# Late experts' one-hot products in fp32r: weighted matrix split high and low, built on GpSimd

## The reference, cut to what matters

```python
def block(xb):
    q = (xb @ w_query).reshape(PEER_TOKEN_BLOCK, PEER_HEADS, 2, D_KEY // 2)
    s = jnp.einsum('thpc,pkc->thpk', q, sub_keys).astype(jnp.float32)
    s1, i1 = lax.top_k(s[:, :, 0], PEER_TOPK)
    s2, i2 = lax.top_k(s[:, :, 1], PEER_TOPK)
    ...
    e = (jnp.take_along_axis(i1, ci // PEER_TOPK, axis=-1) * N_KEYS
         + jnp.take_along_axis(i2, ci % PEER_TOPK, axis=-1))
    g = jax.nn.softmax(sc, axis=-1)
    u = expert_u[e]
    act = jax.nn.gelu(jnp.einsum('td,thkd->thk', xb, u).astype(jnp.float32))
    return jnp.einsum('thk,thkd->td', (g * act).astype(xb.dtype), expert_v[e])
```

## Time and profile before

| what | before |
|---|---|
| runs shown | 1579.97, 1580.24, 1581.9 us; median 1580.24 |
| profiled execution | 1581.13 us, its span 1579.4 us |
| TensorE busy | 1535.6 us, 97% of the span |
| VectorE, ScalarE, GpSimd busy | 1158.2, 834.4, 298.4 us |
| late stage | 982.5 to 1223.6 us |

### The profile page before, as it was taken

One profiled execution on the slowest core, in us unless ns is written; L12 is line 12 of the kernel. 1 busy time (PEld: TensorE's weight loads), 2 busy tenths in 40 slices (PEclk: granted clock), 3 DMA queues, 4 the chain that ended last, 5 costly groups with the idle time before them and its releaser, 6 DMA issues.

```text
span 1579.4 us, 31066 instructions
## 1 busy us (share of the span) xinstructions
PE 1535.6 (97%) x10840; PEld 1431.5 (91%) x10840; DVE 1158.2 (73%) x2379; ACT 834.4 (53%) x1466; POOL 298.4 (19%) x418
## 2 busy tenths in 40 slices
PE   7999999999999999999999998999999999999998
PEld 7998787899899999889999998999999888888886
DVE  5799887765566666875999996888888665666664
ACT  5545678654544445564576675333333545454544
POOL 2010664000100000000000002888887000000000
PEclk9999999999999999999999999999999999999999
DMA  7573433543465554423455554444444656656663
GB/s 247 176 251 105 141 111 118 162 166 126 158 190 177 184 184 147 161 96 105 161 173 168 192 184 150 141 137 140 139 138 147 195 196 189 197 189 197 189 197 107
DMA packets 70860, 257.80 MB, mean 163 GB/s; under 512 B 8272, under 2 KB 8480, under 8 KB 70528
## 3 DMA queue, kind: packets, MB, share of 16 engines
q1 hardware_dynamic: 67824, 246.97, 48.1%
q0 software_dynamic: 2960, 9.86, 2.0%
HBM read 254.67 MB, written 1.08 MB: 162 GB/s over the span
## 4 chain that ended last, share of the span: by engine, by line
PE 84%; DVE 9%; ACT 4%; POOL 1%; issue 1%; DMA 0%; DVEq 0%; ACTq 0%; POOLq 0%
PE bank L362 17%; PE bank L363 17%; PE bank L364 17%; PE bank L940 7%; PE bank L941 7%; PE bank L939 7%; PE bank L918 4%; DVE arena L1642 2%; DVE ring_lo L1561 2%; POOL arena L1007 1%; ACT ring_hi L1065 1%; PE bank L446 1%; ACT arena L1199 1%; PE bank L430 1%; PE bank L432 1%
## 5 line engine op out<-in xcount | busy, mean ns | idle before, releaser
L1561 DVE TENSOR_TENSOR ring_lo<-ring_raw,ring_hi 128x1024 fp32r<-128x1024 f32 x460 | 564.5, 1231 | 187.3 <-ACT ring_hi L1065 184.6
L362 PE MATMUL bank<-operand_hi,ring_hi 128*128 128x256 f32 x2144 | 621.9, 290 | 16.4 <-DVE ring_lo L1561 8.4
L363 PE MATMUL bank<-operand_lo,ring_hi 128*128 128x256 f32 x2144 | 611.1, 285 | 0.0
L364 PE MATMUL bank<-operand_hi,ring_lo 128*128 128x256 f32 x2144 | 611.0, 285 | 0.0
L1065 ACT ACTIVATE ring_hi<-ring_raw 128x1024 fp32r<-128x1024 f32 x460 | 481.7, 1049 | 84.2 <-PE bank L364 70.0
L362 PEld LDWEIGHTS bank<-operand_hi,ring_hi 128*128 128x128 f32 x2144 | 416.3, 194 | 19.5 <-DVE ring_lo L1561 10.8
L363 PEld LDWEIGHTS bank<-operand_lo,ring_hi 128*128 128x128 f32 x2144 | 416.5, 194 | 0.2
L364 PEld LDWEIGHTS bank<-operand_hi,ring_lo 128*128 128x128 f32 x2144 | 415.7, 194 | 0.0
L1049 POOL TENSOR_SCALAR onehots<-iota_k,routeT 128x128 f32<-128x128 f32 x256 | 205.6, 818 | 586.4 <-ACT routeT L1483 544.2
L939 PE MATMUL bank<-ring_hi,hidden_hi 128*128 128x512 f32 x512 | 199.2, 389 | 0.0
L940 PE MATMUL bank<-ring_lo,hidden_hi 128*128 128x512 f32 x512 | 199.2, 389 | 0.0
(11 more groups left out here) (281 smaller groups left out, 1802.8 us busy)
## 6 DMA issues: line engine op xcount, KB each, us to landing
ring_raw<-in_stream SPq DMA_DIRECT2D x467, 512.0 KB, 3.6
arena<-bias_rows POOLq DMA_DIRECT2D x8, 384.0 KB, 4.2
arena<-in_memT SPq DMA_DIRECT2D x2, 512.0 KB, 5.1
arena<-in_xT POOLq DMA_DIRECT2D x1, 1024.0 KB, 9.1
arena<-in_w POOLq DMA_DIRECT2D x2, 512.0 KB, 10.5
arena<-in_memT POOLq DMA_DIRECT2D x1, 1024.0 KB, 5.3
out_rows<-arena SPq DMA_DIRECT2D x2, 512.0 KB, 2.6
arena<-arena POOLq DMA_DIRECT2D x4, 128.0 KB, 4.7
```

The lines of the kernel that those rows point to most:

```text
L362: pe.matmul(out, wh, xh, start=start, stop=False, **kw)
L363: pe.matmul(out, wh, xl, start=False, stop=False, **kw)
L364: return pe.matmul(out, wl, xh, start=False, stop=stop, **kw)
L1561: dve.tensor_tensor(w_lo[:, slot, 0:n], raw[:, slot, 0:n], (raw if n == 1 else w_hi)[:, slot, 0:n].bitcast(F32), ALU.subtract)\
```

## The change

The product is made of two fp32r products. The one-hot of i2 is exact in fp32r, so only the weighted one-hot of i1 is split.

- GpSimd now builds the weighted one-hots (compare and multiply in one instruction with two scalars per partition) into `weighted`, in plain f32. This shares its memory (the tile is named final_gain) with act_out, std, ident and ones_mean.
- ScalarE gets `split_hots(n + 2)`: the high part as fp32r, one instruction of 128x512, into h_hi (even blocks) or h_lo (odd ones). Those are free in this stage. It stands between `hi` and the GELUs and waits for GpSimd.
- VectorE builds the one-hots of i2 (128x512, one instruction) and, when the high part is there, the low part (128x512) in `build_hots`.
- TensorE: per token two products with the same stationary side. It waits for hot_ready alone.
- The copy of the weights of tiles not done moves from VectorE to ScalarE (`rest_of_block`), ahead of `hi`; gate_block waits for it.
- `build_hots` of block 1 is made ahead of the loop, as that of block 0. GpSimd's wait for the products of block n - 2 stays.

```diff
@@ build: tiles @@
-        hot = sb("onehots", [P, 2, TB, P])
+        hot = sb("onehots", [P, 2, TB, P], F32R)
...
+        with ExitStack() as shared:
+            fg = shared.enter_context(nc.sbuf_tensor("final_gain", [P, D], F32))
+        with ExitStack() as shared:
+            act2 = shared.enter_context(nc.sbuf_tensor("act_out", [P, 2, S], F32))
+            std = shared.enter_context(nc.sbuf_tensor("std", [P, S], F32))
+            ident = shared.enter_context(nc.sbuf_tensor("ident", [P, P], F32))
+            ones = shared.enter_context(nc.sbuf_tensor("ones_mean", [P, P], F32))
+        low = sb("weighted_lo", [P, 2, TB, P], F32R)
+        high = [h_hi[:].rearrange("p a (b i) -> p (a b) i", i=NEXP), h_lo[:].rearrange("p a (b i) -> p (a b) i", i=NEXP)]
...
-        row_hot = [[act_hot[:, j, :] for j in range(TB)], [std_hot[:, 0, :], std_hot[:, 1, :], ident[:], ones[:]]]
+        weighted = fg[:].rearrange("p (q t i) -> p q t i", q=2, t=TB)
@@ TensorE, weight_block(n, q, free) @@
                 pe.wait_ge(hot_ready, n + 1)
-                pe.wait_ge(hot_built, n + 1)
                 pe.wait_ge(bank_free[6 + q], free)
                 for j in range(TB):
-                    m = pe.matmul(bank[6 + q][:, j * NEXP:(j + 1) * NEXP], hot[:, q, j, :], row_hot[q][j],
-                                  start=True, stop=True)
+                    o = bank[6 + q][:, j * NEXP:(j + 1) * NEXP]
+                    pe.matmul(o, hot[:, q, j, :], high[q][:, j, :], start=True, stop=False)
+                    m = pe.matmul(o, hot[:, q, j, :], low[:, q, j, :], start=False, stop=True)
@@ GpSimd @@
-                    ins = pool.tensor_scalar(hot[:, q, j, :], iota_k[:], routeT[:, 1, token], None, ALU.is_equal)
+                    ins = pool.tensor_scalar(weighted[:, q, j, :], iota_k[:], routeT[:, 0, token], routeT[:, 2, token], ALU.is_equal, ALU.mult)
@@ ScalarE @@
+            def split_hots(n):
+
+                act.wait_ge(hot_built, n + 1)
+                act.activation(high[n % 2], weighted[:, n % 2, :, :], ACT.Copy).then_inc(hot_split, 1)
+
+            def rest_of_block(n):
+
+                act.wait_ge(wall_ps, n + 1)
+                w = bank[6 + n % 2][:, :].rearrange("p (t i) -> p i t", t=TB)
+                act.activation(wall[:, EARLY + n:NEXP, n * TB:(n + 1) * TB], w[:, EARLY + n:NEXP, :], ACT.Copy).then_inc(rest_kept, 1)
+
+            split_hots(0)
+            split_hots(1)
             for n in range(BLOCKS):
                 q = n % 2
                 gated = TB * (n + 1)
+                rest_of_block(n)
                 hi(u0 + n + 3, (u0 + n + 3) % RING)
+                if n + 2 < BLOCKS:
+                    split_hots(n + 2)
@@ VectorE @@
             def build_hots(n):
 
                 q = n % 2
-                if n >= 2:
-                    dve.wait_ge(wall_ps, n - 1)
-                for j in range(TB):
-                    token = slice(n * TB + j, n * TB + j + 1)
-                    ins = dve.tensor_scalar(row_hot[q][j], iota_k[:], routeT[:, 0, token], routeT[:, 2, token], ALU.is_equal, ALU.mult)
-                ins.then_inc(hot_ready, 1)
+                tokens = routeT[:, 1, n * TB:(n + 1) * TB]
+                dve.tensor_tensor(hot[:, q, :, :], iota_k[:].unsqueeze(1).to_broadcast([P, TB, P]),
+                                  tokens.unsqueeze(2).to_broadcast([P, TB, P]), ALU.is_equal)
+                dve.wait_ge(hot_split, n + 1)
+                dve.tensor_tensor(low[:, q, :, :], weighted[:, q, :, :], high[q].bitcast(F32), ALU.subtract).then_inc(hot_ready, 1)
...
-                dve.tensor_tensor(v, w[:, 0:done, :], v, ALU.mult)
-                dve.tensor_copy(wall[:, done:NEXP, tokens], w[:, done:NEXP, :]).then_inc(bank_free[6 + q], 1)
+                dve.wait_ge(rest_kept, n + 1)
+                dve.tensor_tensor(v, w[:, 0:done, :], v, ALU.mult).then_inc(bank_free[6 + q], 1)
...
             build_hots(0)
+            build_hots(1)
...
-                if n + 1 < BLOCKS:
+                if 1 <= n < BLOCKS - 1:
                     build_hots(n + 1)
```

More of the change, by code:

```diff
@@ L132, in build @@
         gates = at(32194, 3, NH, TT)
-        gates_by_row = act2[0:3 * NH, 0, :]
         vcmp = at(32290, 2, P)
@@ L180, in build @@
         iota_k = sb("iota_k", [P, P])
+        with ExitStack() as shared:
[7 more added lines that the diff above has]
+        high = [h_hi[:].rearrange("p a (b i) -> p (a b) i", i=NEXP), h_lo[:].rearrange("p a (b i) -> p (a b) i", i=NEXP)]
+        gates_by_row = act2[0:3 * NH, 0, :]
         wall = at(0, P, S)
-        act_hot = act2[:].rearrange("p a (b i) -> p (a b) i", i=NEXP)
-        std_hot = std[:].rearrange("p (b i) -> p b i", i=NEXP)
-        row_hot = [[act_hot[:, j, :] for j in range(TB)], [std_hot[:, 0, :], std_hot[:, 1, :], ident[:], ones[:]]]
+        weighted = fg[:].rearrange("p (q t i) -> p q t i", q=2, t=TB)
         fin = at(0, TT, D)
         fsq = at(2048, TT, D)
-        fg = hot[:].rearrange("p q t i -> p (q t i)")
         bank = [ctx.enter_context(nc.psum_tensor(f"bank{b}", [P, 512], F32)) for b in range(8)]
@@ L279, in build @@
         hot_ready = sem("hot_ready")
+        hot_split = sem("hot_split")
+        rest_kept = sem("rest_kept")
         wall_ps = sem("wall_ps")
@@ L1048, in _ @@
                     token = slice(n * TB + j, n * TB + j + 1)
-                    ins = pool.tensor_scalar(hot[:, q, j, :], iota_k[:], routeT[:, 1, token], None, ALU.is_equal)
+                    ins = pool.tensor_scalar(weighted[:, q, j, :], iota_k[:], routeT[:, 0, token], routeT[:, 2, token], ALU.is_equal, ALU.mult)
                 ins.then_inc(hot_built, 1)
             pool.wait_ge(wall_ps, BLOCKS)
-            pool.dma_start(fg, fg_d.to_broadcast([P, D])).then_inc(fg_in, 16)
+            pool.dma_start(fg[:], fg_d.to_broadcast([P, D])).then_inc(fg_in, 16)
         @block.scalar
```

## The result

| | before | after |
|---|---|---|
| median of the runs | 1580.11 us (4 runs, 1579.33 to 1581.9) | 1643.59 us (4 runs, 1643.25 to 1644.59) |
| ratio, 95% interval | | 1.0398 (1.0382 to 1.0413) |
| profiled execution, its span | 1581.13, 1579.4 us | 1643.25, 1641.4 us |

The change costs 63.5 us, against a forecast of 8 and a range that ended at 1606. The direction was right, the size was not.

The account below looks back on a forecast made before the run. The prediction took TensorE to bound the late experts. Products +4, GpSimd hold-up +3 and start +0.9 us summed to +8 us: 1589 us profiled, 1588 us as median, with a range of 1570 to 1606 us.

Parts of the forecast that it names:

- What bounds the kernel: Late experts: TensorE never pauses, 64 blocks of 3.77 us; the stage costs what TensorE needs unless it must wait.
- TensorE, +4 us: Late experts' one-hot products: eight fp32r products at 0.120 us, 0.96 us per block against 0.90, +4 us in 64 blocks.
- quick-load rival: TensorE's one-hot products: fp32r loads are quick, 0.067 us a product, kernel faster, 1566 us; chance 15%.
- VectorE and ScalarE: Late experts: VectorE swaps 1.2 us of work for 1.2 us; ScalarE gains 0.63 and 0.28 us, with 2.3 us free.
- I take 0.60: GpSimd's compare-and-multiply, four per block: 0.60 us each, between 0.24 and 0.84 us, keeping 3.19 us per block.
- The hold-up: GpSimd delayed by VectorE's operations: between 0 and +22 us, taken as 0.05 us per block, +3 us.
- The sentence on the lock: Skill's exclusive lock: every VectorE operation with two SBUF inputs blocks a reading GpSimd, so the sum leans to the upper end.
- The path: Chain from GpSimd over ScalarE and VectorE to TensorE: ready at +7.12 us, due at +7.53, 0.4 us left.
- The two as one case: GpSimd as bound, 15%: held over both operations 1603 us, or 0.84 us per operation 1606; both together 1678, 2%.
- The point given, 3.6 us of GpSimd per block: GpSimd's time per block in the late experts from which the GpSimd-bound rival was said to decide.
- The start, +0.9 us: Start of the late experts: first split and low part delay TensorE's start from 982.50 to near 983.4 us, +0.9 us.

Follow-up runs that it names:

- shared: The change, with GpSimd building two of each block's four weighted one-hots and VectorE the other two: 1581.27 us, against 1581.4 us before.
- swapped builders: The change, with GpSimd comparing for the i2 one-hots and VectorE building the weighted ones and the low part: 1585.32 us, against 1581.4 us before.
- second step alone: The kernel before, with GpSimd's compare given a second step, times an immediate 1.0: 1581.56 us, against 1580.07 us before.
- run without the multiply: The change, with GpSimd only comparing and not multiplying by g, so weights are 0 or 1: 1602.66 us.
- one-input one-hots: The change, with VectorE building the i2 one-hots by four operations with one SBUF input instead of one with two: 1611.55 us.

## Why the prediction was wrong

- **What bounds the kernel**: right. TensorE had no slack in this stage (every variant that keeps it from waiting, and only those, stays at 1581 to 1585 or below), and the cost had to come as a wait before the one-hot products.
- **TensorE, +4 us**: mis-sized. The product measured 0.112 us, the low bound (the load floor), so the term is 0. The choice of 0.120 added a fixed 0.013 us that the product of 128 columns does not show. The runs with shared and with swapped builders show the eight products at no cost. The quick-load rival is out for fp32r. It is what bf16 does: 0.057 us. The 81 ns for pairs of load and matmul with 128 columns from the Trainium skill ("TensorE: Matmul & The Clock Gate", section "Back-to-back issue gap") is met by neither: 0.112 and 0.057 us here. The prediction's estimate by it was also mis-subtracted: 0.65 us for 0.96 per block takes 20 us off its sum, not 16, which is the distance from today's 0.90.
- **VectorE and ScalarE**: right. The one-hots took 0.68, the low part 0.69, the split 0.63 us, and both engines had time to spare. But each was priced by its busy time; that the gating grows over the stage and lengthens GpSimd's round was not in the sum.
- **GpSimd, "I take 0.60"**: this is the step that failed first. The operation measured 0.79 us, near the upper bound of 0.84 (the compare plus half of the multiply). The reason given for 0.60, that the compare stays in it, ignored that the second step is additional work: 0.12 us for it and 0.08 for the second column, by the run with the second step alone.
- **The hold-up**: the second half of the same failure. The chain was worked out for GpSimd held over both operations (4.3 us) and came out at 4.1 us per block. The run without the multiply measured 4.28 and 4.13. But I took 0.05 us per block, near the low end, on the strength of today's 3.19 us, which had been measured with one hold-up; in the change GpSimd is held over both new operations and under the residual split in the block shown, and a block takes 0.97 us more. The sentence on the lock, which spoke for the upper end, moved nothing.
- **The path**: the chain that was priced runs over two blocks and ends with TensorE, with 0.4 us to spare at +7.12 of +7.53. It is the limit of the runs without the multiply and with one-input one-hots (4.1 and 4.2 us). It is not the one that binds in the change. That is the round of one block from GpSimd over ScalarE's GELUs and VectorE's residual split back to GpSimd's held-up operation, 4.56 us early and 5.02 us late in the stage. The prediction had each of its pieces and never closed it.
- **The two as one case**: the prediction priced slow operation and hold-up singly (1606, 1603) and together (1678, "a tail to which I give 2%"). Together is what happened, at 4.74 us per block instead of 5.3. They were treated as independent mishaps. They are not: with 0.59 us per operation four of them take 4.28 us only in every second block and 3.03 us in the other, with 0.79 us nearly every block is held up twice. And they do not add: from 0.59 to 0.79 us per operation the fully held-up block grew from 4.28 to 4.74 us, by 0.46 and not by 4 x 0.19 = 0.76, since an operation that starts later is held up for less. The point given, 3.6 us of GpSimd per block, decides nothing by itself: at 3.77 the kernel before loses nothing (the second step alone), at 7.31 / 2 = 3.66 the change without the multiply loses 23 us. The direction came out right through the hold-up alone, whose mechanism was right and whose size was not; TensorE's +4 us had no part in it.
- **The start, +0.9 us**: right. TensorE waits 1.79 us before its first one-hot product, for 0.91 in the earlier trace rows.

## What to carry to other kernels

Before giving an engine a dearer instruction, price its whole queue per period with every hold-up in it, and do that first; its busy share does not tell the room, since time for which it is held up counts as busy. On GpSimd count each operation of VectorE with two SBUF inputs as a stop of nearly its own length (0.52 us for one of 0.68), even where VectorE itself has time. Then ask what the end of that queue releases: if it sets going the very operations that hold the queue up in the next block, the length of that round is the period, and making any piece of it longer costs every block. And a product whose price is its weight load gets cheaper by a type with a shorter load (bf16 here), not by one that only streams faster.

## What the runs showed of the hardware that was not expected

- GpSimd's tensor_scalar on 128x128: 0.59 us for a compare with a column, 0.71 with a second step by an immediate, 0.79 with a second step by a column. In the cross attention 256 elements took 0.48 us, so the count of elements tells little about the compare.
- A GpSimd operation that is held up by a two-input operation of VectorE ends 0.5 to 0.7 us after the end of that one; two such operations of VectorE in a row hold it over both (1.54 us).
- Two engines can lock each other into a rhythm in this way that neither's free work asks for: 4.56 to 5.02 us per block, with GpSimd's free operations at 0.79 us throughout.
- The 128-column product costs 0.112 us in fp32r and 0.057 us in bf16, with LDWEIGHTS records of 192 and 97 ns.
